# First two weight slabs as plain fp32 with unnormalised x, and probabilities of heads 0 to 14 transposed by VectorE and transfers

## The reference

```python
h = rmsnorm(x, a_norm)
a, b, z = split(h @ a_w_in)                    # 2048 -> 3 x 2048
u = a * sigmoid(b)
c = causal depthwise conv of u, width 31, + a_conv_b
y = silu(layernorm(c)) * silu(z);  x = x + y @ a_w_out
k_g, v_g = split(rmsnorm(x, kv_norm) @ w_kv)   # three groups, 16 heads of 128
q_g, z = split(rmsnorm(x, b_norm) @ b_w_in)
# group g: window/dilation (128,1), (512,4), (2048,16)
s = q_g k_g^T / sqrt(128) + bias(distance), masked
o = one softmax over the groups' scores, merged by denominators, times v_g
x = x + (o * silu(z)) @ b_w_out;  out = rmsnorm(x, final_norm)
```

## Time and profile before

| | us |
|---|---|
| median of 3 runs | 1428.08 (1427.71 to 1428.09) |
| profiled execution | 1427.84 |
| its span | 1426.0 |
| PE busy | 1414.5 (99%), 8515 instructions |
| DVE busy | 866.0 (61%) |
| ACT busy | 705.3 (49%) |
| POOL busy | 387.2 (27%) |
| DMA, queue of SP | 65.9% of 16 engines, 277.47 MB |

### The profile page before, as it was taken

One profiled execution on the slowest core, in us unless ns is written; L12 is line 12 of the kernel. 1 busy time (PEld: TensorE's weight loads), 2 busy tenths in 40 slices (PEclk: granted clock), 3 DMA queues, 4 the chain that ended last, 5 costly groups with the idle time before them and its releaser, 6 DMA issues.

```text
span 1426.0 us, 22807 instructions
## 1 busy us (share of the span) xinstructions
PE 1414.5 (99%) x8515; PEld 1256.6 (88%) x8515; DVE 866.0 (61%) x1417; ACT 705.3 (49%) x999; POOL 387.2 (27%) x171
## 2 busy tenths in 40 slices
PE   8999999999999999999999999999999999999997
PEld 8999999988888888888888888888888888888886
DVE  3999999632544444446666666666656666666523
ACT  6444444675644444445454545444444544545543
POOL 6888888888300000000000000000000000001595
PEclk9999999999999999999999999999999999999999
DMA  9766766655757557569676676666577666574662
GB/s 283 195 183 187 195 180 192 193 177 180 242 202 254 201 198 253 196 201 265 191 196 183 172 194 197 184 184 185 164 207 194 177 185 185 161 220 151 229 207 88
DMA packets 401023, 279.06 MB, mean 196 GB/s; under 512 B 6731, under 2 KB 355483, under 8 KB 400588
## 3 DMA queue, kind: packets, MB, share of 16 engines
q1 hardware_dynamic: 400492, 277.47, 65.9%
q10 hardware_dynamic: 480, 0.90, 0.2%
HBM read 267.79 MB, written 10.55 MB: 195 GB/s over the span
## 4 chain that ended last, share of the span: by engine, by line
PE 98%; ACT 1%; DMA 0%; DVE 0%; issue 0%; POOL 0%; POOLq 0%; ACTq 0%
PE bank L423 14%; PE bank L419 14%; PE bank L447 10%; PE bank L449 10%; PE bank L448 10%; PE bank L422 7%; PE bank L420 7%; PE bank L427 6%; PE bank L428 6%; PE bank L429 6%; PE bank L1521 1%; PE bank L1559 1%; PE bank L1413 1%; PE bank L1539 0%; PE bank L1544 0%; ACT mem_a L699 0%
## 5 line engine op out<-in xcount | busy, mean ns | idle before, releaser
L365 POOL TENSOR_TENSOR w_lo<-raw,w_hi 128x1024 fp32r<-128x1024 f32 x159 | 382.7, 2423 | 1013.1 <-ACT w_hi L356 1013.0
L356 ACT ACTIVATE w_hi<-raw 128x1024 fp32r<-128x1024 f32 x254 | 268.4, 1061 | 326.4 <-PE bank L449 192.5
L394 DVE TENSOR_TENSOR w_lo<-raw,w_hi 128x1024 fp32r<-128x1024 f32 x224 | 272.2, 1223 | 111.6 <-ACT w_hi L388 109.1
L388 ACT ACTIVATE w_hi<-raw 128x1024 fp32r<-128x1024 f32 x224 | 236.5, 1058 | 155.1 <-PE bank L423 147.1
L427 PE MATMUL bank<-mem_a,w_hi 128*128 128x256 f32 x768 | 216.1, 281 | 1.8 <-DVE mem_a L1012 1.6
L428 PE MATMUL bank<-mem_a,w_hi 128*128 128x256 f32 x768 | 214.4, 279 | 0.0
L429 PE MATMUL bank<-mem_a,w_lo 128*128 128x256 f32 x768 | 213.4, 278 | 0.0
L423 PE MATMUL bank<-mem_b,w_hi 128*128 128x512 f32 x512 | 202.5, 396 | 0.0
L419 PE MATMUL bank<-mem_b,w_hi 128*128 128x512 f32 x512 | 202.3, 395 | 0.0
L365 DVE TENSOR_TENSOR w_lo<-raw,w_hi 128x1024 fp32r<-128x1024 f32 x96 | 117.6, 1226 | 135.0 <-ACT w_hi L356 134.9
L447 PE MATMUL bank<-w_hi,mem_a 128*128 128x512 f32 x504 | 196.5, 390 | 0.0
(11 more groups left out here) (195 smaller groups left out, 2106.6 us busy)
## 6 DMA issues: line engine op xcount, KB each, us to landing
raw<-b_w_in_dram SPq DMA_DIRECT2D x128, 512.0 KB, 4.3
raw<-w_kv_dram SPq DMA_DIRECT2D x48, 1024.0 KB, 7.0
raw<-w_kv_dram SPq DMA_DIRECT2D x96, 512.0 KB, 5.5
raw<-a_w_in_dram SPq DMA_DIRECT2D x47, 1024.0 KB, 5.8
raw<-a_w_out_dram SPq DMA_DIRECT2D x16, 1024.0 KB, 5.0
raw<-b_w_out_dram SPq DMA_DIRECT2D x16, 1024.0 KB, 5.0
v_dram<-v_stage SPq DMA_DIRECT2D x12, 512.0 KB, 3.4
v_rows<-v_dram SPq DMA_DIRECT2D x15, 384.0 KB, 5.8
```

The lines of the kernel that those rows point to most:

```text
L356: nc.scalar.activation(w_hi[:, stream.half_slot(half), :], raw[:, slot, part:part + HALF], ACT.Copy).then_inc(hi_done, 1)
L365: eng.tensor_tensor(w_lo[:, stream.half_slot(half), :], raw[:, slot, part:part + HALF], w_hi[:, stream.half_slot(half), :].bitcast(F32), A ...
L394: nc.vector.tensor_tensor(w_lo[:, QKV.half_slot(half), :], raw_half(half), w_hi[:, QKV.half_slot(half), :].bitcast(F32), ALU.subtract).the ...
```

## The change

Start. x is loaded in four column quarters and slabs 0 and 1 in four pieces each. TensorE does 16 warm-up transposes, transposes raw x, and multiplies slabs 0 and 1 as plain fp32 (one product, two passes, for three split ones) with x that has only the gain applied, as each quarter arrives. The row factor r0 = 1/rms is made beside it, turned into a row by two diagonal products, and applied to the results of slabs 0 and 1 in the first gating (glu(0)) and to x itself (x_hat), whose hi and lo parts serve all later slabs. The bias table's product moves behind slab 2. Loads of the first loop turn wait until slabs 0 and 1 are multiplied.

Heads. VectorE transposes the normalised probabilities in 32 x 32 squares (two instructions a head), and SP moves the squares to their places in the other partitions by 16 transfers of 32 KB, back into prob. hi and lo of the first group are made from there, and the products of the other groups read prob directly. attend follows one head behind instead of two. Head 15 still goes over TensorE.

After the loop, attend(14) is no longer in B_OUT, and ScalarE's order is another.

```diff
-NORM_PIECES, WARM_UP = 4, 48
+QUARTERS, WARM_UP = 4, 16
-PEELED = 3
+PEELED = 2
@@ SP, start
+            load_x(0)
+            for n in range(2):
+                load_piece(n, 0)
+            for q in range(1, QUARTERS):
+                load_x(q)
+            for q in range(1, QUARTERS):
+                for n in range(2):
+                    load_piece(n, q)
...
+            sp.wait_ge(mm_done, 4)
+            sp.wait_ge(first_lo, 1)
@@ SP, heads
+            def move_squares(h):
+                sp.wait_ge(squares_turned, TT * (h + 1))
+                for i in range(SQUARES):
+                    for j in range(SQUARES):
+                        row = BLOCKS * SQUARE
+                        sp.dma_start(prob[j * SQUARE:(j + 1) * SQUARE, :, i * row:(i + 1) * row],
+                                     prob_sq[i * SQUARE:(i + 1) * SQUARE, :, j * row:(j + 1) * row]
+                                     ).then_inc(prob_turned, 16)
                     load_half(sp, h, half, w[:, tiles, bass.ds(cols[half // 2], P)])
+                    if half == NG:
+                        move_squares(h - 2)
@@ ScalarE, heads
+            def probs_hi(h):
+                act.wait_ge(prob_turned, 16 * MOVES * (h + 1))
+                for u in range(TT):
+                    for t in range(TT):
+                        nc.scalar.activation(of_squares(prob_hi[:, u, t * P:(t + 1) * P]),
+                                             turned_probs(t, SAME if t == u else CROSS), ACT.Copy).then_inc(prob_his, 1)
-                if j == NG and stage >= 2:
-                    copy_probs(h - 2)
-                if j == 5 and stage >= 2:
-                    values_hi(h - 2, v_rows, v_loaded, 16 * (h - 1))
+                if j == 5 and stage >= 1:
+                    values_hi(h - 1)
+                if j == 6 and stage >= 1:
+                    probs_hi(h - 1)
@@ ScalarE, after the loop
             exps(last)
-            split_hi(act, B_OUT, 0, 2)
-            y2_his([last - 2])
-            copy_probs(last)
-            values_hi(last, v_last, v_last_in, 16)
-            split_hi(act, B_OUT, 0, 3, halves=(0,))
             y2_his([last - 1])
-            split_hi(act, B_OUT, 0, 3, halves=(1,))
+            values_hi(last)
+            split_hi(act, B_OUT, 0, 2, halves=(0,))
+            act.wait_ge(last_turned, 1)
+            # (copy of prob_hi, two copies of bank 5 into prob)
+            split_hi(act, B_OUT, 0, 2, halves=(1,))
+            split_hi(act, B_OUT, 0, 3)
             y2_his([last])
@@ VectorE, start
+            copy_turned(range(KT - 2))
+            dve.wait_ge(x_squared, TT * QUARTERS)
+            nc.vector.tensor_reduce(sq_sum, sq_part, AX.X, ALU.add).then_inc(x_summed, 1)
+            # (reciprocal of std, two diagonals, r0 from bank 4)
+            make_x_hat(quarter(0))
+            make_x_hat(quarter(1))
+            x_lo(0)
+            make_x_hat(quarter(2))
+            split_lo(dve, AB, 0, 2, first_lo, halves=(0,))
+            x_lo(1)
+            make_x_hat(quarter(3))
+            x_lo(2)
+            x_lo(3)
@@ VectorE, heads
+            def turn_squares(h):
+                positive(dve, prob_turned, 16 * MOVES * h)
+                for t in range(TT):
+                    dve.wait_ge(prob_ready, 2 * h + t + 1)
+                    nc.vector.transpose(prob_sq[:, t, :].rearrange("p (j b s) -> p b j s", j=SQUARES, b=BLOCKS),
+                                        prob[:, t, :].rearrange("p (b j s) -> p b j s", b=BLOCKS, j=SQUARES)
+                                        ).then_inc(squares_turned, 1)
                     normalise(h - 1)
+                    turn_squares(h - 1)
@@ TensorE, start
+            turn_x(0)
+            for q in range(QUARTERS):
+                for kt in range(q * QKT, (q + 1) * QKT):
+                    mm = first_products(0, kt)
...
+                for kt in range(q * QKT, (q + 1) * QKT):
+                    if kt == QKT + 2:
+                        pe.wait_ge(rstd_ready, 1 + TT)
+                        pe.wait_ge(xt_copied, 2 * QKT)
+                        # (two diagonal products into bank 4)
+                    mm = first_products(1, kt)
+                if q == 0:
+                    for n in range(1, QUARTERS):
+                        turn_x(n)
@@ TensorE, heads
+                    pe.wait_ge(prob_turned, 16 * MOVES * (h + 1))
+                    pe.wait_ge(prob_split, TT * TT * (h + 1))
-                if stage >= 2:
-                    attend(h - 2, v_rows)
                 if stage >= 1:
-                    turn_probs(h - 1)
+                    attend(h - 1)
                 scores(h)
```

More of the change, by code:

```diff
@@ L642, in _ @@
             nc.gpsimd.memset(bias_vec, MASKED).then_inc(vec_masked, 1)
[L644 to L655, removed]
+            nc.gpsimd.memset(stat[:, 31:32], 0.0).then_inc(lo_pool, 5)
+            split_lo(pool, AB, 0, 2, lo_pool, halves=(1,))
+            split_lo(pool, AB, 0, 3, lo_pool)
             with pool.Fori(1, KT // 2) as i:
@@ new lines, in _, with first_w_hi, x_hi @@
+            nc.scalar.activation(std, sq_sum, ACT.Sqrt, bias=eps, scale=1.0 / D).then_inc(std_ready, 1)
+            def first_w_hi(half, j):
+                act.wait_ge(raw_in[j] if j == 3 or half else first_in, 16)
+                nc.scalar.activation(w_hi[:, AB.half_slot(2 * j + half), :], raw[:, j, half * HALF:(half + 1) * HALF],
+                                     ACT.Copy).then_inc(hi_done, 1)
+            def x_hi(q):
+                act.wait_ge(x_hat, q + 1)
+                nc.scalar.activation(parts_a(quarter(q), 0), parts_a(quarter(q), 1, False),
+                                     ACT.Copy).then_inc(in_hi, 1)
@@ new lines, in _ @@
+            for kt in range(KT - 2, KT):
+                act.wait_ge(x_turned, KT // 2)
+                act.wait_ge(a_norm_ready, 1)
+                nc.scalar.activation(of_parity(xt[:, kt, :]), halves(raw_turned(kt)), ACT.Copy,
+                                     scale=vector(A_NORM, kt)).then_inc(xt_copied_act, 1)
+            x_hi(0)
+            first_w_hi(0, 2)
+            x_hi(1)
+            first_w_hi(1, 2)
+            x_hi(2)
+            x_hi(3)
+            for half in range(2):
+                first_w_hi(half, 3)
@@ L1007, in _ @@
[L1007 to L1015 removed]
+            dve.wait_ge(a_rows_turned, 1)
@@ new lines, in _, with copy_turned, make_x_hat @@
+            nc.vector.tensor_copy(vectors[:, A_NORM, :], bank[7][:, 0:KT]).then_inc(a_norm_ready, 1)
+            dve.wait_ge(a_norm_ready, 1)
+            def copy_turned(tiles):
+                for kt in tiles:
+                    dve.wait_ge(x_turned, kt // 2 + 1)
+                    nc.vector.tensor_scalar(of_parity(xt[:, kt, :]), halves(raw_turned(kt)), vector(A_NORM, kt), None,
+                                            ALU.mult).then_inc(xt_copied, 1)
+            def make_x_hat(kts):
+                if kts.start == KT - QKT:
+                    dve.wait_ge(xt_copied, KT - 2)
+                    dve.wait_ge(xt_copied_act, 2)
+                nc.vector.tensor_tensor(parts_a(kts, 1, False), xt[:, kts, :], by_r0(kts),
+                                        ALU.mult).then_inc(x_hat, 1)
@@ L1605, in _ @@
                     if c == 0 and q == 1:
-                        attend(last - 1, v_rows)
-                        turn_probs(last)
+                        turn_last()
                     if c == 0 and q == 2:
-                        attend(last, v_last)
+                        attend(last, True)
             out_project_last(pe, B_OUT, bank[2:4], y2_in, b_first_done)
```

340 lines of the change are left out of this document (183 added, 157 removed).

## The result

| | median us | runs | lowest to highest |
|---|---|---|---|
| before | 1427.89 | 4 | 1427.38 to 1428.09 |
| after | 1416.82 | 4 | 1415.44 to 1417.10 |

Ratio 0.9921, 95% interval 0.9908 to 0.9933: 11.1 us faster. The forecast was 1414.7, the range 1411.5 to 1420. The profiled execution of the kernel after took 1416.98 us with a span of 1415.2; against the span of 1426.0 before, that is 10.8 less. The trace divides this into the prediction's three parts.

The account below looks back on a forecast made before the run. TensorE was taken to bound the kernel, busy for all 558 us of the head loop. 1427.84 - 13.1 (heads) - 2.2 (start) + 2.2 (after the loop) = 1414.7 us; range 1411.5 to 1420.

Parts of the forecast that it names:

- TensorE is the bound: Head loop: TensorE busy every microsecond, so removing 15 heads' transposes at 0.88 us gains 13.2, taken as 13.1.
- The products that read prob in runs of 32 columns: attend in the heads: this form taken at the dense pace, no change, with ends 0 and +0.05 us per head.
- VectorE's transposes at 1.3: Each head, after normalise: two 128x512 transposes on VectorE taken at 1.3 us, between ends of 0.88 and 2.4.
- The transfers, forecast at 0.375 to issue: SP in each head: 16 transfers of 32 KB, 6.0 us of issue, all issued by 833, last landed at 836.
- the cover of 10.5: Each head: probs_lo done at about 838.5, attend asks at 849.1; 10.5 us remain, so cost 0 for TensorE.
- The rival that starves the loop: Heads: transfers following each other at over about 1.04 us make TensorE wait; 1451 at 1.2 us each; chance 0.10.
- the rival's rule: Heads with slow transfers: beyond r = 1.04 us per transfer, each head is longer by 16 x (r - 1.04).
- Part 3: After the loop: ScalarE's new order makes TensorE wait once for w_lo in the first output chunk; +2.2 us, ends 0 and +3.
- Part 2: The start: plain fp32 slabs 0 and 1 by quarters bring slab 3 earlier; -2.2 us, ends -3.4 to -1.
- the walk: The start, step by step across engines: slab 2 and the bias product end at 32.6, 2.7 us early.
- the rival of the late rise: Start: TensorE's low pace lasts over the first eight products, 3.6 us more, 1418.3; sign against: no gap over 0.3 before 7; chance 0.14.
- The reserve of 0.5: Start: 2.2 taken of 2.7 us early, leaving 0.5 for waits between engines that were counted at nothing.

Follow-up runs that it names:

- experiment 6: Kernel after with 32 transfers of 16 KB a head for 16 of 32 KB, the same bytes; 1549.66 us, ratio 1.0852.
- experiment 3: Kernel after, with both halves of output slab 2 split on ScalarE before the wait for the last transposes; 1413.57 us, ratio 0.9900.
- experiment 2: Kernel before with only the start's hunks of the change, heads and output as before; 1426.61 us, ratio 0.9994.
- experiment 7: Kernel after with one of the 16 transfers a head, the other 15 squares left unmoved; 1416.21 us, ratio 0.9915.
- experiment 1: Kernel before with only the hunks of the heads and of what follows the loop, the old start kept; 1417.50 us, ratio 0.9931.
- experiment 5: Kernel after, VectorE making both halves of slab 2's w_lo, POOL starting on slab 3 only once x_lo is done; 1415.02 us, ratio 0.9909.
- experiment 4: Kernel after with 24 warm-up transposes for 16; 1416.20 us, ratio 0.9917.
- experiment 8: Kernel after with both halves of output slab 2 split before the wait, VectorE making both w_lo halves of slab 2, 20 warm-ups; 1412.70 us, ratio 0.9895.

## Why the prediction was right, and where not

**TensorE is the bound, and an instruction taken from it is worth its pace: right.** 13.2 was worked out, 13.1 taken, 13.0 measured.

**The products that read prob in runs of 32 columns cost nothing: right.** Eight of attend's hold TensorE for 0.90 (806.54 to 807.44 in its timeline), as eight dense ones of the same size did, and no head is longer than it should be.

**VectorE's transposes at 1.3: right.** Two took 1.29. probs_lo, forecast at 1.4 for four, took 0.90.

**The transfers, forecast at 0.375 to issue: wrong in size, without effect.** They took 0.64, so all were issued at 836.3 for 833, and ScalarE waited 5.71 for some 3. ScalarE's row in order of time, kernel after:

```profile
837.64 0.91 ACT L956 ACTIVATE prob_hi<-prob 128x128 fp32r<-128x128 f32 x4 [5.71 <-DMA prob<-prob_sq]
```

VectorE ended probs_lo at 839.5 for 838.5, so 8.6 of the cover of 10.5 were left for attend, which starts at 848.07. I had taken the price of one form of transfer, a load from DRAM, for another. The range between 0.375 and 1.06 held it. The load on the DMA engines was underrated too: the prediction added 7% by bytes, and their busy share rose from 0.65 to 0.76.

**The cover: taken at the wrong place.** The prediction measured it to attend. The scores ask for q_t, and VectorE makes that behind probs_lo. In the kernel after:

```profile
838.59 0.90 DVE L1332 TENSOR_TENSOR prob_lo<-prob,prob_hi 128x128 fp32r<-128x128 f32 x4 [5.86 <-ACT prob_hi L956]
...
843.43 2.35 DVE L431 TENSOR_TENSOR w_lo<-raw,w_hi 128x1024 fp32r<-128x1024 f32 x2
845.70 0.42 DVE L1309 TENSOR_TENSOR q_t<-bank,lower_odd 128x256 f32<-128x256 f32 x1
```

q_t is done at 846.1 and the scores start at 849.67, so the cover was 3.6 in this head (2.8 to 4.5 over all heads), and not 8.6. It held, so cost 0 came true, with less to spare than was forecast.

**The rival that starves the loop: a real mechanism, and its place was half right.** The rate did not come near the 1.04 from which it was to decide, but experiment 6 brings the same load by doubling the count: 20.2 of issue for 10.3 is 9.9 more, and spends attend's 8.6 of cover and 1.3 more. attend then waits 1.2, as the rival's rule says. What the rival did not have is what stands behind probs_lo on VectorE: w_lo, and q_t, for which the scores ask. By their cover of 3.6 the two waits together should be 9.9 - 3.6 = 6.3 a head; measured are 1.2 + 4.8 = 6.0. The idle time brings the clock down as well: 8.9 a head where the rival's rule with attend's cover gives 1.3. The loop would so begin to lose from some (10.3 + 3.6)/16 = 0.87 us for each transfer (an estimate from these two traces), not from 1.04. The prediction's own two sums for 1.06 differ as well: probs_lo at 847.5 leaves 1.6 before attend, the rival's rule has 0.3 lost. One adds 1 us for the last landing, the other 3. The rule of the Trainium skill, "DMA: Bandwidth & Descriptors", "Rules for kernel authors", against transfers under 64 KB fits as a rule on count (the pace did not change with the bytes from 32 to 16 KB); no run has more than 32 KB in this form, so its limit is not tested. The 2.0 us in series did not come: one landed 1.9 after its issue in the median, but they overlapped, one every 0.64. That page's anatomy section, moreover, is about transfers that GpSimd issues, and these are issued by SP.

**Part 3: right.** 1.9 to 2.1 for 2.2, on the forecast chain; experiment 3 removes it.

**Part 2 is the step that failed, and the reason for 1416.8 in place of 1414.7.** It was forecast at -2.2 and is +0.2 in the profiled execution, -1.1 in the median of experiment 2. The forecast of the whole is 2.1 us off, and nearly all of that lies here. Against the walk, which put slab 3 at 32.6 before its reserve of 0.5, the trace has 2.8 more, in three terms:
- x's first quarter was taken at 5.0; it landed at 6.13, and the transposes ended 0.95 later than in the walk. The walk had taken little more than the shortest time to landing, 4.0 after an issue at 0.7, of the loads of x in the kernel before, whose median was 5.5.
- The first eight products took 4.85 for 3.6: +1.25. This is the rival of the late rise, at a third of its price, since the pace rose after some of them and not after all. Its sign against, no gap over 0.3 before 7, did not hold: TensorE stood for 0.45 before 6.17. The views' granted clock reads 1.00 throughout, so it is the spacing that shows it:

```profile
8.00:10.00 2.00, 2.00 (x6) 1.65 (x6) 1.07 (x3) 0.77 (x3) 0.00 (x0) 1.00 1.06 407
10.00:12.00 2.00, 2.00 (x10) 1.70 (x9) 0.00 (x0) 1.88 (x5) 0.00 (x0) 1.00 1.12 334
```

  The start of the kernel after ran unchanged in four experiments. Slab 3 begins at 33.71 and 33.35 where the rise came at 5.32 and 6.09 (experiments 2 and 6; in the latter x was there half a microsecond earlier as well), at 34.07 for 7.95 (experiment 3), at 35.13 for 10.07 (experiment 7) and at 35.43 for 10.60 (kernel after). So with an early rise part 2 gives 1.6 to 1.9 of its forecast 2.2. Forecast and rival are two outcomes of one start, where the prediction had them as alternatives. How much of the spread between runs this makes is not shown: each kernel has one trace, and experiment 1 has two groups of runs with the old start.
- Slab 2 and the bias product took 8.0 for 6.67: +1.4. The walk counted nine instructions of 1.22 on VectorE and let POOL work beside it free. Experiment 5 shows that it was not free: 2.2 longer for one x_lo, of which slab 2 and the bias product paid 1.1.
- The wait for r0, the diagonals and the remaining products were 0.7 shorter than in the walk, together.

The reserve of 0.5 for what a walk has at nothing was too small for a stretch where four engines and the first loads depend on each other within a microsecond. The lower end of the gain given there, 1 us, fits experiment 2; the kernel after in its profiled execution lies beyond it.

## What to carry to other kernels

Where TensorE is busy in every microsecond of a loop, moving its transposes to VectorE and to transfers within SBUF is worth their full time, as long as the wait that it adds leaves cover for everything queued behind it on each engine, and not only for the instruction that is waited for: here 3.6 us were left, not the 8.6 before the next reader of the moved data. Count such transfers and not their bytes, and take their price from the same form. Forecast a start of some 30 us with a wide range: a gain of 2 us there was smaller than the sum of one late load, one late rise of TensorE's pace and one meeting of two engines. Where a view gives a clock of 1.00 at the very start, look at the spacing of like instructions before believing it.

## What the runs showed of the hardware

- A subtraction of two SBUF tiles on VectorE took 3.39 us for 1.22 when POOL was in one of its own. Experiments 3, 4 and 7 have the same 3.39, and in experiments 5 and 8 it is gone. In experiment 5 the gating (u) met POOL's subtraction instead and took 1.41 for 0.49.
- An issue of a transfer from SBUF to SBUF took 0.63 to 0.67 us on SP, at 16 and at 32 KB, alone or in a row of 16 or 32. In a row it landed 1.8 to 1.9 after its issue in the median (up to 3.5), alone 3.7 (experiment 7).
- TensorE's pace at the start rose at another moment in each of the ten traces, between 4.60 and 10.60 us: with 48 warm-ups at 6.83 (before) and 7.30 (experiment 1), with 24 at 6.24, with 20 at 4.60, with 16 at 5.32, 6.09, 7.95, 10.07, 10.36 (experiment 5) and 10.60. Until 4.60 all ten ran the same transposes without a pause, so that work alone doesn't decide the moment. In the six traces in which TensorE had not paused before the rise, it came by 7.30. In the four in which it had (the kernel after, experiments 3, 5 and 7, with a wait of 0.36 to 0.68 for x after 5.4), it came at 7.95 or later. One trace for each kernel suggests that the pause matters, and does not show it.
- When TensorE stood idle for 5.3 of the 10 us from 874 to 884 (experiment 6), the granted clock fell to 0.66 in the mean of the last six and products took 0.41 for 0.28: 5.9 us of idle time in a head cost 2.9 more.
